# Gated delta rule on one NeuronCore: k's norm and beta are added to the gates' exponent, and the query term stands behind the exponents

## What is computed

```python
def l2_normalize(x):
    xf = x.astype(jnp.float32)
    return xf * lax.rsqrt(jnp.sum(xf * xf, -1, keepdims=True) + EPS)

def gated_delta_rule(q, k, v, g, beta, S0):
    ...
    Gc = jnp.cumsum(gc, axis=-1)
    decay = jnp.exp(jnp.where(incl, Gc[..., :, None] - Gc[..., None, :], -jnp.inf))
    kk = jnp.einsum('...id,...jd->...ij', kc, kc)
    M = jnp.eye(C, dtype=jnp.float32) + jnp.where(strict, bc[..., :, None] * kk * decay, 0.0)
    gam = jnp.exp(Gc)
    W = lax.linalg.triangular_solve(M, (bc * gam)[..., None] * kc, left_side=True, lower=True, unit_diagonal=True)
    U = lax.linalg.triangular_solve(M, bc[..., None] * vc, left_side=True, lower=True, unit_diagonal=True)
    qk = jnp.einsum('...id,...jd->...ij', qc, kc) * decay
    q_dec = gam[..., None] * qc
    k_dec = jnp.exp(Gc[..., -1:] - Gc)[..., None] * kc
    g_last = jnp.exp(Gc[..., -1])
    ...
        u_ = U_ - jnp.einsum('bhck,bhkv->bhcv', W_, S)
        o_ = jnp.einsum('bhck,bhkv->bhcv', qd_, S) + jnp.einsum('bhij,bhjv->bhiv', qk_, u_)
        S = gl_[..., None, None] * S + jnp.einsum('bhck,bhcv->bhkv', kd_, u_)

def gdn_mixer(h, conv_buf, S0, w_in, conv_w, a_log, dt_bias, o_norm, w_out):
    ...
    q = l2_normalize(conv[..., :HK].reshape(B, T, GDN_HEADS, GDN_DK)) * (GDN_DK ** -0.5)
    k = l2_normalize(conv[..., HK:2 * HK].reshape(B, T, GDN_HEADS, GDN_DK))
    v = conv[..., 2 * HK:].reshape(B, T, GDN_HEADS, GDN_DV)
    g = -jnp.exp(a_log.astype(jnp.float32)) * jax.nn.softplus(a.astype(jnp.float32) + dt_bias.astype(jnp.float32))
    beta = jax.nn.sigmoid(b.astype(jnp.float32))
    o, S = gated_delta_rule(q, k, v, g, beta, S0)
    o = rms_norm(o, o_norm) * jax.nn.silu(z.astype(jnp.float32).reshape(B, T, GDN_HEADS, GDN_DV))
```

## Time and profile before

| | us |
|---|---|
| time, median of 3 runs | 1335.26 |
| lowest and highest run | 1334.72, 1336.23 |
| the profiled execution's own time | 1334.86 |
| its span, first to last instruction | 1332.9 |
| granted TensorE clock, share of full speed | 0.998 |
| PE busy | 1309.3 |
| VectorE, ScalarE, GpSimd busy | 634.4, 507.1, 365.9 |

### The profile page before, as it was taken

The page is one execution under the profiler, slowest core; times in us unless marked ns, Lnnn a source line. Parts: engine busy times, 40 slices in busy tenths (PEclk is TensorE's granted clock), DMA queues, the critical chain, the costliest instruction groups (busy, mean ns, idle before and its releaser), DMA issues.

```text
span 1332.9 us, 28024 instructions
## 1 busy us (share of the span) xinstructions
PE 1309.3 (98%) x11596; PEld 1086.3 (81%) x11596; DVE 634.4 (48%) x1009; ACT 507.1 (38%) x785; POOL 365.9 (27%) x506
## 2 busy tenths in 40 slices
PE   8999999999999999999999999999999999999997
PEld 7766588888888888887778777877888888888886
DVE  5447653333333322267776677766633333332222
ACT  6243453222222322244555465545432223222221
POOL 1004324121212100165453545453221222211010
PEclk9999999999999999999999999999999999999999
DMA  8658422422232232111212221122223222233211
GB/s 264 209 191 278 143 96 95 149 102 99 94 122 104 101 121 85 63 64 40 89 41 88 88 72 57 73 96 66 96 105 116 94 94 94 94 118 131 88 44 64
DMA packets 32140, 140.89 MB, mean 106 GB/s; under 512 B 4634, under 2 KB 6938, under 8 KB 20155
## 3 DMA queue, kind: packets, MB, share of 16 engines
q1 hardware_dynamic: 32058, 139.75, 30.2%
HBM read 128.63 MB, written 11.11 MB: 105 GB/s over the span
## 4 chain that ended last, share of the span: by engine, by line
PE 92%; DVE 4%; ACT 1%; issue 1%; DMA 1%; SPq 0%; DVEq 0%; ACTq 0%
PE P L1745 64%; PE P L2110 10%; PE P L2303 2%; DVE wl L1486 1%; PE P L2288 1%; PE P L2365 1%; PE P L2296 1%; PE P L2119 1%; PE P L1823 1%; PE P L2125 1%; PE P L2331 1%; PE P L2345 1%; PE P L1955 1%; PE P L2321 1%; PE P L1898 1%
## 5 line engine op out<-in xcount | busy, mean ns | idle before, releaser
L1745 PE MATMUL P<-zh,wh 128*128 128x260 f16 x1712 | 329.2, 273 | 2.1 <-DVE wl L1194 2.1
L1745 PE MATMUL P<-zl,wh 128*128 128x260 f16 x1712 | 329.0, 273 | 0.0
L1745 PE MATMUL P<-zh,wl 128*128 128x260 f16 x1712 | 329.0, 273 | 0.0
L1174 DVE SCALAR_TENSOR_TENSOR wl<-stage,wh 128x2048 f16<-128x2048 f32 (+1 forms) x75 | 185.3, 2471 | 195.4 <-ACT wh L761 192.8
L1745 PE MATMUL P<-arena,wh 128*128 128x260 f16 x1816 | 276.2, 273 | 1.0 <-DVE hT L1391 0.3
L1745 PEld LDWEIGHTS P<-arena,wh 128*128 128x128 f16 x1816 | 175.0, 97 | 29.2 <-issue 1.3
L1745 PEld LDWEIGHTS P<-zh,wh 128*128 128x128 f16 x1712 | 164.3, 97 | 34.0 <-issue 6.7
L1745 PEld LDWEIGHTS P<-zh,wl 128*128 128x128 f16 x1712 | 165.6, 97 | 25.9
L1745 PEld LDWEIGHTS P<-zl,wh 128*128 128x128 f16 x1712 | 165.4, 97 | 25.8
L1745 PE MATMUL P<-arena,wl 128*128 128x260 f16 x908 | 174.5, 273 | 0.0
L761 ACT ACTIVATE wh<-stage 128x2048 f16<-128x2048 f32 (+1 forms) x80 | 161.8, 2023 | 3.6 <-PE P L1745 3.6
(11 more groups left out here) (366 smaller groups left out, 1646.3 us busy)
## 6 DMA issues: line engine op xcount, KB each, us to landing
stage<-w_gu SPq DMA_DIRECT2D x44, 1024.0 KB, 4.8
stage<-w_in SPq DMA_DIRECT2D x23, 1024.0 KB, 4.9
stage<-w_dn SPq DMA_DIRECT2D x16, 1408.0 KB, 5.8
arena<-cache_k SPq DMA_DIRECT2D x32, 256.0 KB, 3.5
stage<-w_out SPq DMA_DIRECT2D x8, 1024.0 KB, 5.4
arena<-cache_v SPq DMA_DIRECT2D x32, 256.0 KB, 3.0
arena<-delta_state SPq DMA_DIRECT2D x8, 512.0 KB, 3.5
o_ds<-arena SPq DMA_DIRECT2D x8, 512.0 KB, 6.8
```

Source lines behind the costliest of these rows:

```text
L1174: nc.vector.scalar_tensor_tensor(out=wl[:, j, 0:words], in0=stage[:, j, 0:words], scalar=WS, in1=wh[:, j, 0:words], op0=MUL, op1=SUB).then ...
L1745: mm = nc.tensor.matmul(pm[j][:, c, :], w[:, wslot, o:o + 128], x[:, k, c * CH:(c + 1) * CH], start=(k == first and w is wh and x is xh), ...
```

## The change

k is no longer normalised. Its squared norm is taken from the diagonal of k times k instead: PE computes k against k as the first step of a head (kk_ps, now without beta), VectorE multiplies each of the four squares with the identity and sums along rows (dg, into ksq), ScalarE takes the logarithm (klog). The rows of beta now hold -log beta, formed with the gate's rows at the stage's start; after the transposition into tokens VectorE adds it to the gate once (tokg). In a head tj = tokg + klog is subtracted from the gate of each column, so that the exponent of et also carries beta and the squared norm; d4 likewise. bV takes the factor kn, the norm, in place of beta. For the decode tokens an extra small product with ones sums q k and k k (qkk, 16 columns), and ScalarE forms rk, the reciprocal norm, that VectorE uses with beta. Both of norm_l2's ScalarE passes, GpSimd's square and its product, PE's stat_l2, VectorE's k times beta and the selection of beta over 512 columns go. A part takes stat_l2's place at chunk 2 of heads 0 to 6, and one fewer stands behind chunk 0. The query term of head h - 1 moves from ahead of the exponents to behind them, and gam moves on ScalarE behind the identity copy. On GpSimd the gamma product on k comes ahead of the six copies.

```diff
     "pe": ...
-    "act": ["gam", "gd", "et", "kd4", "yi", "ye", "nf", "kd", "x"] + ["ye", "x"] * 4 + ["bv", "ye", "x"] + ["u"] * 4 + ["o"],
-    "dve": ["ex", "bd", "kb", "nt", "xt", "at"] + ["z", "xt"] * LEVELS + ["s"] + ["r", "s"] * 3,
-    "pool": ["selb"] + ["om"] * LEVELS + ["kbg", "qd"],
+    "act": ["gd", "lr", "lk", "rk", "kn", "et", "kd4", "yi", "gam",
+            "ye", "nf", "kd", "x"] + ["ye", "x"] * 4 + ["bv", "ye", "x"] + ["u"] * 4 + ["o"],
+    "dve": ["dg", "ex", "bd", "nt", "xt", "at"] + ["z", "xt"] * LEVELS + ["s"] + ["r", "s"] * 3,
+    "pool": ["selb", "kbg"] + ["om"] * LEVELS + ["qd"],
...
+            def decode_products(h):
                 pool.wait_ge(csilu, 3 * h + 2)
                 if h >= 1:
+                    pool.wait_ge(kqs_ps, h)
+                    pool.wait_ge(*G("gb_ps", h))
+                q, k = qkvc[:, h % 2, 0, SEQ:], qkvc[:, h % 2, 1, SEQ:]
+                nc.gpsimd.tensor_copy(kd2, two(k))
...
+                nc.gpsimd.tensor_tensor(qkk[:, 0:8], q, k, MUL)
+                nc.gpsimd.tensor_tensor(qkk[:, 8:16], k, k, MUL).then_inc(dprep, 1)
...
             for h in range(HG):
                 p, n = h + 1, h - 1
                 act.wait_ge(*G("gb_ps", h + 1))
-                nc.scalar.activation(gamB, P[:, 2, :], ACT.Exp).then_inc(S["gam"], 1)
                 nc.scalar.activation(gD[:, h, :], P[:, 7, 0:8], ACT.Exp).then_inc(S["gd"], 1)
+                nc.scalar.activation(rk, P[:, 7, 24:32], ACT.Ln, bias=epsc[:, 2:3]).then_inc(S["lr"], 1)
+                act.wait_ge(*G("dg", h + 1))
+                nc.scalar.activation(klog, ksq, ACT.Ln, bias=epsc[:, 2:3]).then_inc(S["lk"], 1)
+                act.wait_ge(*G("lr", h + 1))
+                nc.scalar.activation(rk, rk, ACT.Exp, scale=-0.5)
+                nc.scalar.activation(qks, P[:, 7, 16:24], ACT.Copy).then_inc(S["rk"], 1)
+                act.wait_ge(*G("lk", h + 1))
+                nc.scalar.activation(kn, klog, ACT.Exp, scale=0.5).then_inc(S["kn"], 1)
                 act.wait_ge(*G("ex", h + 1))
                 nc.scalar.activation(et, et, ACT.Exp).then_inc(S["et"], 1)
                 nc.scalar.activation(kd4, d4, ACT.Exp).then_inc(S["kd4"], 1)
...
+                nc.scalar.activation(gamB, P[:, 2, :], ACT.Exp).then_inc(S["gam"], 1)
                 next_split("in1", h, 1)
...
-                dve.wait_ge(*G("gd", h + 1))
-
+                dve.wait_ge(*G("kk_ps", h + 1))
+                for c in range(4):
+                    ins = nc.vector.tensor_tensor_reduce(out=dg_out[c], in0=P[:, 6, c * 128:(c + 1) * 128], in1=ident[:, :],
+                                                         scale=1.0, scalar=0.0, op0=MUL, op1=ADD,
+                                                         accum_out=ksq[:, c:c + 1])
+                ins.then_inc(S["dg"], 1)
+                dve.wait_ge(*G("lk", h + 1))
+                link(nc.vector.tensor_tensor(tj, tokg[:, :, h], klog, ADD))
                 for c in range(4):
                     nc.vector.scalar_tensor_tensor(out=et[:, c * 128:(c + 1) * 128], in0=P[:, 2, c * 128:(c + 1) * 128],
-                                                   scalar=tokm[:, c, h:h + 1], in1=msk[:, 1, :], op0=SUB, op1=MIN)
...
+                                                   scalar=tj[:, c:c + 1], in1=msk[:, 1, :], op0=SUB, op1=ADD)
...
+                nc.vector.tensor_tensor(br, P[:, 7, 8:16], rk, MUL).then_inc(S["bd"], 1)
+                if n >= 0:
+                    add_query(n)
                 convolve(h, 2, 0)
...
+                pe.wait_ge(csilu, 3 * h + 2)
+                if h >= 1:
+                    pe.wait_ge(*G("u", 4 * h))
+                chunks(6, k, k, "kk_ps")
                 ready(h, "selb")
...
                 fill(4 if h < HG - 1 else 3)
                 if h >= 1:
-                    pe.wait_ge(nln, h + 1)
+                    pe.wait_ge(snew, h)
                     stat_head(h - 1)
-                pe.wait_ge(nq, h + 1)
-                ready(h, "kb")
...
-                chunks(6, k, kbg_w, "kk_ps")
-                ready(h, "gd", "bd")
+                ready(h, "gd", "rk", "bd")
                 chunks(7, k, q, "qk_ps")
...
-                        if c == 2:
+                        if c == 2 and h == HG - 1:
                             pe.wait_ge(snew, h + 1)
-                            if h + 1 < HG:
-                                stat_l2(h + 1)
-                            else:
-                                stat_query()
+                            stat_query()
                         else:
                             fill(1)
...
                     if c == 0:
-                        fill(3)
+                        fill(2 if h < HG - 1 else 3)
```

More of the change, by code:

```diff
@@ L201, in hybrid_trunk @@
         qq = [sq[:, 0, :], rs2[:, 0, :]]
-        gD, bD = (a2(64).rearrange("p (h b) -> p h b", h=HG) for _ in range(2))
+        tokg = rs2[:, 1, 0:32].rearrange("p (c n) -> p c n", c=4)
+        ksq, klog, kn, tj = (rs2[:, 1, 32 + 4 * i:36 + 4 * i] for i in range(4))
+        rk, br, qks = (rs2[:, 1, 48 + 8 * i:56 + 8 * i] for i in range(3))
+        gD = a2(64).rearrange("p (h b) -> p h b", h=HG)
         gate = a2(8)
@@ L2083, in _ @@
             unit("in1", 0, 1, zh, zl)
-            def stat_l2(h):
-                pe.wait_ge(nsq, h + 1)
-                for c in range(2):
-                    mm = nc.tensor.matmul(stat[:, c, :], ones[:, :], sq[:, 1, c * CH:(c + 1) * CH],
-                                          start=True, stop=True)
-                mm.then_inc(nstat, 1)
             def stat_head(h):
@@ L2143, in stat_last @@
                 mm.then_inc(o1stat, 1)
[L2145 removed]
             pe.wait_ge(rows_ready, 2)
             for c in range(4):
[L2149 removed]
+                mm = nc.tensor.transpose(P[:, 5, 40 * c:40 * c + 40], rows[0:40, c * 128:(c + 1) * 128],
                                          ident[0:40, 0:40])
@@ L2220, in _ @@
                 if h == 0:
-                    for m in range(2):
-                        nc.tensor.matmul(P[:, 2 + m, :], selb[0:40, m, :], rows[0:40, 0:SEQ], start=True, stop=True)
+                    nc.tensor.matmul(P[:, 2, :], selb[0:40, 0, :], rows[0:40, 0:SEQ], start=True, stop=True)
                     for m in range(2):
@@ L2228, in _ @@
                         pe.wait_ge(rows3, 3)
-                    for m, t in enumerate((g3, b3)):
-                        nc.tensor.matmul(P[:, 2 + m, :], sel3[0:72, h % 2, :], t[0:72, 0:SEQ], start=True, stop=True)
+                    nc.tensor.matmul(P[:, 2, :], sel3[0:72, h % 2, :], g3[0:72, 0:SEQ], start=True, stop=True)
                     ready(h - 1, "o")
@@ L2266, in between @@
                                              start=True, stop=True)
-                        nc.tensor.matmul(P[:, 4, 256:264], ones[:, :], qkp, start=True, stop=True)
                         nc.tensor.transpose(P[0:36, 4, 264:392], kpad[:, 0:36], ident[:, :]).then_inc(kqs_ps, 1)
```

102 lines of the change are left out of this document (38 added, 64 removed).

## The result

The changed kernel takes **1339.22 us** (median of 10 runs, 1337.44 to 1340.57) against 1335.28 (10 runs) for the kernel before on the same chip: ratio 1.0025, 95% interval 1.0015 to 1.0035. It is slower, by 3.9 us: little, but the interval excludes 1. The profiled execution took 1339.27, with a span of 1337.6.

The account below looks back on a forecast made before the run. PE, busy 98% of the span, was taken as the bound. Heads 1 to 6 + 3.1, head 7 + 1.5 and head 0 - 0.5 gave + 4.1 us: about 1339.3 us for the median, range 1332.5 to 1344.

Parts of the forecast that it names:

- The addition is held, 1.4 us: Head's start: VectorE's addition tj, both operands in SBUF, waits for GpSimd's state decay; bounds 0 and 1.4 us, 1.4 taken.
- the first rival: The addition at the head's start isn't held by GpSimd's decay: 5.6 us less than forecast, 1329.7, faster; chance 0.12.
- et + 1.87: Head's start: ScalarE's exponential et starts at 772.15 instead of 770.28, 1.87 us later.
- L1068/L2296 + 2.04: ScalarE's scaled copy of the transposed k ends 2.04 us later, and so does PE's transpose behind it.
- The query statistic waits 1.7, and this costs nothing: Head's start: PE waits about 1.7 us for VectorE's query term; not added, since PE still waits later.
- L2296 still waits 0.8: PE works on to 779.5 and its transpose still waits 0.8 us for ScalarE's scaled copy.
- End of a head - 0.97: Heads 0 to 6: 0.31 us less at chunk 2 and 0.67 less behind chunk 0, together 0.97 less.
- Level 1 - 0.55: Earlier GpSimd products free VectorE's second split of level 1; PE's wait goes, 0.55 us less, bounds 0 and 0.85.
- A steady head + 0.52: Heads 1 to 6: 2.04 - 0.97 - 0.55 = + 0.52 us each, + 3.1 together.
- Head 0 - 0.5: Head 0: - 0.97 at its end, + 0.5 taken at its start; together - 0.5 us.
- Head 7 + 1.5: Last head: no saving at its end, so 2.04 - 0.55 = + 1.5 us.
- The clock is no term: TensorE's clock was taken as granted at 2.4 GHz throughout (0.998), also at small waits; no time added.

Follow-up runs that it names:

- e1: Changed kernel, but the logarithm read by VectorE's 128x4 addition is written to PSUM, with a second logarithm in SBUF for k's norm: 1330.95 us, ratio 0.9966.
- e2: Changed kernel, but GpSimd's state decay waits until VectorE has written the exponents' arguments; addition untouched: 1337.18 us, ratio 1.0017 to the kernel before.
- e4: Changed kernel, but VectorE's query term stands ahead of the four reductions again: 1341.82 us, ratio 1.0052 to the kernel before.
- e5: Changed kernel, but GpSimd's gamma product stands behind the six copies again: 1341.30 us, ratio 1.0036 to the kernel before.
- e9: Changed kernel, with one projection part of heads 0 to 6 moved from the head's start to behind chunk 0: 1385.98 us, ratio 1.0365.
- e3: Changed kernel with four projection parts instead of three ahead of the query statistic in head 7: 1345.09 us, ratio 1.0069.

## Why the prediction was right, point by point

The forecast was 1339.3 for the median; 1339.22 was measured. The hold, which decides the sign, is confirmed by e1 and e2. That the number fits to 0.1 us is luck: heads 1 to 6 grew by 1.6 us less than worked out, head 7 by 1.3 more and head 0 by 0.3 more.

- **The addition is held, 1.4 us.** Right, and a little over-sized: it lasts 1.35 in seven heads and 0.16 unheld, so the hold is 1.2. Its end is within 0.02 of the decay's; e1 and e2 show that the decay is the cause and that the operand's place decides. e1, with the hold taken out, took 1330.95; the first rival, the same kernel unheld, had 1329.7.
- **et + 1.87.** Over-sized: + 1.67 (5.01 us behind the end of the last head's products, against 3.34). The decay starts 1.83 behind it, where the working had 1.92, and the addition ends with the decay and not 0.10 after it.
- **L1068/L2296 + 2.04.** Over-sized with it: + 1.74 (13.21 against 11.47). gam's 0.48 less the idle 0.31 should have put 0.17 between et and the scaled copy; it is 0.06 (6.91 us from 772.88 to 779.79, against 6.85 in the earlier trace rows). The nf evacuation, L1045 before and L1032 now, starts 0.34 us behind the start of the operation ahead of it, where it was 0.74: this gives 0.40 back and not 0.31.
- **The query statistic waits 1.7, and this costs nothing.** Right: 1.57, and e4 shows that the time is only waited later. **L2296 still waits 0.8**: 0.65.
- **End of a head - 0.97.** The 0.67 behind chunk 0 is right. At chunk 2 the gap is 1.00 where 0.89 was worked out (the earlier trace rows had 1.20): 0.20 and not 0.31, because the first two passes behind a wait take 0.33 and not 0.22.
- **Level 1 - 0.55.** 5.35 us from the transposes to level 2, against 5.90: right, and e5 shows that just over half of it hangs on the product's place.
- **A steady head + 0.52.** The trace gives 1.74 - 0.55 - 0.88 = + 0.31. The six heads together grew by 1.5 and not 3.1: head 1 grew not at all, since it had taken 44.22 before, with 0.5 us of waiting at its first product that is gone.
- **Head 0 - 0.5.** It was - 0.16, from the end of the projection ahead of it. The hold of L1589 (now L1595) by decay and gamma product in turn was named, but priced as if PE would not notice; e5 shows 0.8 us for it.
- **Head 7 + 1.5, "The clock is no term".** This is the step that failed. It was + 2.8, and 1.25 of that came with the fall of the clock. The working knew that PE waits 1.7 us for the query term and that head 7 has three parts instead of four, and didn't add the two: a wait of 2.2. It argued from the granted clock at the small waits of the kernel before, while the change itself made the waits longer. In their mean clock the ten runs fall into two groups: the two with 0.999 took 1337.4 us, the eight with 0.996 or 0.997 took 1339.1 to 1340.6. A mean of 0.999 leaves no room for more than the clock's fall at the kernel's end, which takes 3.5 to 6.3 us in the traces. So in two of ten runs the clock seems to have stayed up in head 7, with the same instructions. The mean doesn't say where it fell: runs of the kernel before with 0.996 took 1337.3 to 1337.5.

The heads' differences add up to 4.2 us (- 0.16, + 1.52, + 2.82). The spans differ by 4.7: the other 0.5 is there before layer 1 begins, within the first 31 us, where the two kernels do the same work. Its cause is open. What follows the last head takes 392.9 us in both.

## What to carry to other kernels

A tiny operation on the path to a waiting engine was priced here by its operands' places, not by its size: look for what GpSimd has in flight, and move one operand to PSUM rather than move GpSimd's work, which in e2 only found the next operations of VectorE. When a change makes the bounding engine wait longer, add up the wait in the head that has the least cover, and ask of it whether the clock will still be granted behind it. Filler work cut into parts has its own evacuations; a part moved by one place moves them all.

## What was not expected of the hardware

- The clock. At the head's start a wait of 1.57 us left it at 2.4 GHz, and behind one of 2.24 us it was at 1.2 GHz for most of the next 3.8 us, in seven heads of e9 and in head 7 of the changed kernel and of e5. In e3 it fell behind 1.47 us (PE busy 0.71 of the 2 us from 922) and not behind 2.16 us (PE busy 0.51 of the 2 us from 910). What decides between them is open.
- The price of it: 1.25 us for a fall at a head's start and 0.75 for one in level 0. Of the 47 us of e9 these falls are about 12 (seven times 1.25 and four times 0.75, an estimate that leaves out one fall late in head 1). PE's waits in head 4 add up to 5.6 us, against 2.2 in the changed kernel.
- A hold works on one-operand work too: VectorE's 128x512 multiplication by one number per partition (L1446) took 2.12 us beside the decay instead of 0.48. It works the other way as well: the decay took 2.35 and 2.12 instead of 1.90 when it started beside VectorE's query term (e2, e4).
